# Conv stage: two halves of the gated product and one half of b turned by VectorE blocks and a DRAM round trip

## What is computed

```python
def short_conv_mixer(x, w_in, conv_w, w_out):
    b, c, v = jnp.split(x @ w_in, 3, axis=-1)
    y = b * causal_depthwise_conv(c * v, conv_w)      # 3 taps along the tokens
    return y @ w_out
# h = h + rms_norm(mix); w_in is 1024 x 3072, w_out 1024 x 1024
```

## Time and profile before

| | |
|---|---|
| profiled execution, its own time | 1416.56 us |
| its span, first to last instruction | 1414.8 us |
| median of the timed runs | 1417.77 us |
| PE busy | 1392.3 us, 98% of the span |
| VectorE (DVE) busy | 1026.2 us, 73% |
| ScalarE (ACT) busy | 1011.9 us, 72% |
| GpSimd (POOL) busy | 68.9 us, 5% |
| granted TensorE clock, mean | 0.999 |
| conv stage, its part of the span | about 500 to 585 us |

### The profile page before, as it was taken

The page is one execution under the profiler, slowest core; times in us unless marked ns, Lnnn a source line. Parts: engine busy times, 40 slices in busy tenths (PEclk is TensorE's granted clock), DMA queues, the critical chain, the costliest instruction groups (busy, mean ns, idle before and its releaser), DMA issues.

```text
span 1414.8 us, 20634 instructions
## 1 busy us (share of the span) xinstructions
PE 1392.3 (98%) x7859; PEld 1142.9 (81%) x7859; DVE 1026.2 (73%) x1417; ACT 1011.9 (72%) x1826; POOL 68.9 (5%) x163
## 2 busy tenths in 40 slices
PE   6999999999999999999999999999999999999998
PEld 5888888888888887788887888887778888788886
DVE  5878788777666766676667766677989886876665
ACT  7657574748777554587875977767888886588784
POOL 8000000000000000000000000001030300000000
PEclk9999999999999999999999999999999999999999
DMA  7542453345656555565655565646453432566562
GB/s 234 166 142 91 145 200 121 119 149 180 201 186 206 180 190 181 158 207 188 205 181 179 195 202 185 203 157 194 129 163 112 118 123 90 165 208 200 187 206 91
DMA packets 168291, 238.27 MB, mean 168 GB/s; under 512 B 21554, under 2 KB 114640, under 8 KB 168192
## 3 DMA queue, kind: packets, MB, share of 16 engines
q1 hardware_dynamic: 166496, 233.57, 51.1%
q0 software_dynamic: 1632, 3.35, 0.8%
q10 hardware_dynamic: 64, 0.02, 0.0%
HBM read 235.07 MB, written 1.84 MB: 167 GB/s over the span
## 4 chain that ended last, share of the span: by engine, by line
PE 93%; ACT 3%; DVE 2%; DMA 1%; issue 1%; SPq 0%; DVEq 0%; ACTq 0%
PE A L245 17%; PE A L246 17%; PE A L247 17%; PE M L247 5%; PE G L246 5%; PE M L246 5%; PE G L247 5%; PE M L245 5%; PE G L245 5%; PE A L1325 1%; PE G L1246 1%; PE G L1293 1%; DVE tmp L414 1%; PE M L1303 1%; ACT w_hi L209 1%; DVE x_lo L419 1%
## 5 line engine op out<-in xcount | busy, mean ns | idle before, releaser
L227 DVE TENSOR_TENSOR w_lo<-raw,w_hi 128x1024 fp32r<-128x1024 f32 (+2 forms) x296 | 506.8, 1726 | 128.7 <-ACT w_hi L209 128.0
L209 ACT ACTIVATE w_hi<-raw 128x1024 fp32r<-128x1024 f32 (+2 forms) x296 | 426.7, 1462 | 120.9 <-DMA raw<-in_ffn_w_gate_up 93.3
L245 PE MATMUL A<-w_hi,x_hi 128*128 128x512 f32 (+1 forms) x640 | 258.7, 404 | 3.6 <-DVE x_lo L419 1.0
L247 PE MATMUL A<-w_hi,x_lo 128*128 128x512 f32 (+1 forms) x640 | 247.1, 386 | 0.0
L246 PE MATMUL A<-w_lo,x_hi 128*128 128x512 f32 (+1 forms) x640 | 246.5, 385 | 0.0
L690 ACT ACTIVATE ffn_ffn_hT<-ffn_ffn_hb 32x128 f32<-32x128 f32 x576 | 176.9, 307 | 15.6 <-DVE ffn_ffn_hb L755 2.5
L245 PEld LDWEIGHTS A<-w_hi,x_hi 128*128 128x128 f32 x640 | 120.2, 188 | 33.5 <-DVE x_lo L419 6.8
L247 PEld LDWEIGHTS A<-w_hi,x_lo 128*128 128x128 f32 x640 | 120.1, 188 | 25.1
L245 PE MATMUL A<-w_hi,ffn_ffn_hT_hi 128*128 128x512 f32 x352 | 139.0, 395 | 0.0
L246 PE MATMUL A<-w_lo,ffn_ffn_hT_hi 128*128 128x512 f32 x352 | 138.4, 393 | 0.0
L246 PEld LDWEIGHTS A<-w_lo,x_hi 128*128 128x128 f32 x640 | 120.5, 188 | 21.0 <-issue 0.7
(11 more groups left out here) (392 smaller groups left out, 2018.5 us busy)
## 6 DMA issues: line engine op xcount, KB each, us to landing
raw<-in_ffn_w_gate_up SPq DMA_DIRECT2D x176, 512.0 KB, 4.8
raw<-in_ffn_w_down SPq DMA_DIRECT2D x88, 512.0 KB, 4.0
raw<-in_w_in SPq DMA_DIRECT2D x48, 512.0 KB, 4.2
raw<-in_gdn_w_in SPq DMA_DIRECT2D x48, 512.0 KB, 4.6
raw<-in_sc_w_in SPq DMA_DIRECT2D x24, 512.0 KB, 4.3
raw<-in_w_out SPq DMA_DIRECT2D x16, 512.0 KB, 4.5
raw<-in_gdn_w_out SPq DMA_DIRECT2D x16, 512.0 KB, 4.0
raw<-in_w_mem_kv SPq DMA_DIRECT2D x8, 512.0 KB, 5.9
```

What stands on the lines that cost most here:

```text
L209: ins = act.activation(net.w_hi[:, v % RING, part], net.raw[:, v % RING, part], ACT.Copy)
L227: ins = dve.tensor_tensor(net.w_lo[:, v % RING, part], net.raw[:, v % RING, part], net.w_hi[:, v % RING, part].bitcast(F32), ALU.subtract)
L245: pe.matmul(out, xh, hi[:, k, c, :], start=start and k == 0, stop=False)
L247: mm = pe.matmul(out, xl, hi[:, k, c, :], start=False, stop=stop and k == nk - 1)
```

## The change

Three of the four turns leave TensorE: c*v of both halves and b of half 0. For each of them VectorE turns the 32x32 blocks of the tile in place (new step `tb`, one instruction on 128x1024 elements); GpSimd then writes the tile to a scratch tensor in DRAM (512 KB, 4 KB a partition), waits for it, and reads it back with four DMAs, one for each 32 partitions, each of 1024 runs of 32 floats, which puts the blocks in place. ScalarE's and VectorE's taps and the product with b then read SBUF instead of the banks G and M. The step order changes: `turncv:0` moves behind unit 7, `mul:0` into v1, `turncv:1` behind unit 11 and still ahead of `b:1`. The fourth turn (b of half 1) stays on TensorE but is made in the middle of unit 12, between its second and third quarter, and TensorE's wait for `b_out(2)` moves there with it; units 12 and 13 are written as quarters for this. ScalarE's `b:1` waits for `y(2)` instead of `b_turned(2)`, VectorE's `cv:1` for `tapped(2)` and its own chain.

```diff
+        self.by_blocks = [("cv", 0), ("b", 0), ("cv", 1)]
+        self.blocks, self.turned_in, self.turned_out = s("blocks"), s("turned_in"), s("turned_out")
+        self.turned_dram = net.scratch_dram(f"{name}_turned", [len(self.by_blocks), P, TT * 512])
...
-        steps = "unit:c:0:0 unit:c:0:1 c:0 unit:v:0:0 unit:v:0:1 cv:0 unit:b:0:0 turncv:0 unit:b:0:1 b:0 " \
-                "unit:c:1:0 turnb:0 mul:0 unit:c:1:1 c:1 unit:v:1:0 unit:v:1:1 cv:1 unit:b:1:0 turncv:1 " \
-                "unit:b:1:1 b:1 turnb:1 mul:1 out"
+        steps = "unit:c:0:0 unit:c:0:1 c:0 unit:v:0:0 unit:v:0:1 cv:0 tb:cv:0 unit:b:0:0 unit:b:0:1 b:0 tb:b:0 " \
+                "unit:c:1:0 unit:c:1:1 turncv:0 c:1 unit:v:1:0 mul:0 unit:v:1:1 cv:1 tb:cv:1 unit:b:1:0 unit:b:1:1 " \
+                "turncv:1 b:1 turnb:1 mul:1 out"
...
-        self.b = net.sb("sc_b", [P, TT, 512])
-        self.cvs = net.sb("sc_cv", [P, TT, 512])
+        self.b = net.sb("sc_b", [P, 4, TT, P])
+        self.cvs = net.sb("sc_cv", [P, 4, TT, P])
...
     def pool(self, pool):
         self.post.pool(pool)
+        for n, (what, half) in enumerate(self.by_blocks):
+            tile = self.cvs if what == "cv" else self.b
+            pool.wait_ge(*self.blocks(n + 1))
+            pool.dma_start(self.turned_dram[n], tile[:, :, :, :].rearrange("p k t n -> p (k t n)"))\
+                .then_inc(self.turned_out.sem, 16)
+            pool.wait_ge(*self.turned_out(16 * (n + 1)))
+            src = self.turned_dram[n].rearrange("(i c) (m b n) -> b c m i n", i=4, b=4, n=32)
+            for b in range(4):
+                pool.dma_start(tile[32 * b:32 * b + 32, :, :, :].rearrange("p k t (i n) -> p (k t) i n", i=4), src[b])\
+                    .then_inc(self.turned_in.sem, 16)
+
+    def arrived(self, what, half):
+        return self.turned_in(64 * (self.by_blocks.index((what, half)) + 1))
...
+            elif kind in ("turncv", "turnb") and (kind[4:], int(step[1])) in self.by_blocks:
+                continue
+            elif kind in ("turncv", "turnb") and step != ("turnb", "1"):
+                self.turn(pe, kind, int(step[1]))
             elif kind == "out":
                 pe.wait_ge(*self.cv(2))
-                pe.wait_ge(*self.b_out(2))
                 for h in range(2):
-                    pe.wait_ge(*self.y_lo_ready(h + 1))
-                    w.unit(self.y_hi, self.y_lo, 2 * h, 2, 512, [net.A[0:2], net.A[2:4]], h == 0, False, pieces=2)
+                    for q in range(4):
+                        if (h, q) == (0, 2):
+                            pe.wait_ge(*self.b_out(2))
+                            self.turn(pe, "turnb", 1)
+                        if (h, q) in ((0, 0), (1, 0)):
+                            pe.wait_ge(*self.y_lo_ready(h + 1))
+                        w.unit(self.y_hi, self.y_lo, 2 * h, 2, 512, [net.A[0:2], net.A[2:4]], h == 0, False, pieces=2,
+                               quarter=q)
                 w.last_units(self.post, [(self.y_hi, self.y_lo, 2 * h, self.y_lo_ready(h + 1)) for h in (2, 3)])
...
+    def turn(self, pe, kind, half):
+        net = self.net
+        src, banks, sem, ready = (self.cvs, net.G, self.cv_turned, self.cv) if kind == "turncv" \
+            else (self.b, net.M, self.b_turned, self.b_out)
+        pe.wait_ge(*ready(half + 1))
+        if half:
+            pe.wait_ge(*self.y(2))
+        else:
+            pe.wait_ge(*self.pre.lo(4))
+        for pair in range(2):
+            for kk in range(2):
+                for tt in range(TT):
+                    k = 2 * pair + kk
+                    mm = pe.transpose(banks[pair][:, kk * T + tt * P:kk * T + (tt + 1) * P],
+                                      src[:, k, tt, :], net.ident[:, :])
+            mm.then_inc(sem.sem, 1)
...
+    def turns(self, what, half):
+        return 2 * half if (what, 0) not in self.by_blocks else 0
+
+    def cv_of(self, half, pair):
+        if ("cv", half) in self.by_blocks:
+            return self.cvs[:, 2 * pair:2 * pair + 2, :, :].rearrange("p k t n -> p k (t n)")
+        return self.net.G[pair][:, :].rearrange("p (k n) -> p k n", k=2)
...
                 if kind == "c" and half:
                     act.wait_ge(*self.cv(1))
                 if kind == "b" and half:
-                    act.wait_ge(*self.b_turned(2))
+                    act.wait_ge(*self.y(2))
                 for tt in range(TT):
-                    ins = act.activation((self.c if kind == "c" else self.b)[:, tt, :],
-                                         self.banks(n)[tt][:, :], ACT.Copy, scale=net.r[:, tt:tt + 1])
+                    if kind == "c":
+                        dst, src = self.c[:, tt, :], self.banks(n)[tt][:, :]
+                    else:
+                        dst, src = self.b[:, :, tt, :], self.banks(n)[tt][:, :].rearrange("p (k n) -> p k n", k=4)
+                    ins = act.activation(dst, src, ACT.Copy, scale=net.r[:, tt:tt + 1])
                 ins.then_inc((self.c_out if kind == "c" else self.b_out).sem, 1)
+                moved = ("cv", half) in self.by_blocks
                 for pair in range(2):
-                    act.wait_ge(*self.cv_turned(2 * half + pair + 1))
+                    act.wait_ge(*(self.arrived("cv", half) if moved else self.cv_turned(self.turns("cv", half) + pair + 1)))
...
-                                             net.G[pair][:, kk * T:(kk + 1) * T], ACT.Copy,
+                                             self.cv_of(half, pair)[:, kk, :], ACT.Copy,
...
                 dve.wait_ge(net.unit_used, self.u0 + 2 * (n + 1))
                 dve.wait_ge(*self.c_out(half + 1))
                 if half:
-                    dve.wait_ge(*self.cv_turned(2))
+                    dve.wait_ge(*self.tapped(2))
+                    w.chain.sync()
                 for tt in range(TT):
-                    ins = dve.scalar_tensor_tensor(out=self.cvs[:, tt, :], in0=self.banks(n)[tt][:, :],
-                                                   scalar=net.r[:, tt:tt + 1], in1=self.c[:, tt, :],
+                    ins = dve.scalar_tensor_tensor(out=self.cvs[:, :, tt, :],
+                                                   in0=self.banks(n)[tt][:, :].rearrange("p (k n) -> p k n", k=4),
+                                                   scalar=net.r[:, tt:tt + 1],
+                                                   in1=self.c[:, tt, :].rearrange("p (k n) -> p k n", k=4),
                                                    op0=ALU.mult, op1=ALU.mult)
                     if tt == 0:
                         w.chain.mark(ins)
                 ins.then_inc(self.cv.sem, 1)
+            elif kind == "tb":
+                what, half = step[1], int(step[2])
+                dve.wait_ge(*(self.cv if what == "cv" else self.b_out)(half + 1))
+                w.chain.sync()
+                tile = (self.cvs if what == "cv" else self.b)[:, :, :, :].rearrange("p k t n -> p (k t n)")
+                dve.transpose(tile, tile).then_inc(self.blocks.sem, 1)
...
-                                out=row, in0=net.G[pair][:, kk * T:(kk + 1) * T - back],
+                                out=row, in0=self.cv_of(half, pair)[:, kk, 0:T - back],
...
-                    dve.wait_ge(*self.b_turned(n + 1))
-                    dve.tensor_tensor(t, t, net.M[pair][:, :], ALU.mult).then_inc(self.y.sem, 1)
+                    if ("b", half) in self.by_blocks:
+                        dve.wait_ge(*self.arrived("b", half))
+                        b = self.b[:, 2 * pair:2 * pair + 2, :, :].rearrange("p k t n -> p (k t n)")
+                    else:
+                        dve.wait_ge(*self.b_turned(self.turns("b", half) + pair + 1))
+                        b = net.M[pair][:, :]
+                    dve.tensor_tensor(t, t, b, ALU.mult).then_inc(self.y.sem, 1)
```

More of the change, by code:

```diff
@@ L1775, in pe @@
                 w.unit(net.x_hi, net.x_lo, 4 * h, 4, 512, [[b0], [b1]], h == 0, h == 1)
-            elif kind in ("turncv", "turnb"):
-                half = int(step[1])
-                src, banks, sem, ready = (self.cvs, net.G, self.cv_turned, self.cv) if kind == "turncv" \
-                    else (self.b, net.M, self.b_turned, self.b_out)
-                pe.wait_ge(*ready(half + 1))
-                if half:
-                    pe.wait_ge(*self.y(2))
-                else:
-                    pe.wait_ge(*self.pre.lo(4))
-                for pair in range(2):
-                    for kk in range(2):
-                        for tt in range(TT):
-                            k = 2 * pair + kk
-                            mm = pe.transpose(banks[pair][:, kk * T + tt * P:kk * T + (tt + 1) * P],
-                                              src[:, tt, k * P:(k + 1) * P], net.ident[:, :])
-                    mm.then_inc(sem.sem, 1)
+            elif kind in ("turncv", "turnb") and (kind[4:], int(step[1])) in self.by_blocks:
+                continue
+            elif kind in ("turncv", "turnb") and step != ("turnb", "1"):
```

(1 more changed line is left out.)

## The result

The changed kernel takes 1427.15 us, median of 4 runs (1426.23 to 1429.58), against 1417.89 (1417.53 to 1418.14) for the kernel before, measured beside it: a ratio of 1.0073, 95% interval 1.006 to 1.0085. It is slower by 9.3 us, on the side to which the prediction gave 0.39, and just outside its range.

What follows compares the result with a forecast made beforehand. TensorE (PE), 93% of the chain, bounds the kernel. A 4.4 us wait for b1 eats the 4.2 us gained, leaving +0.3; a 0.9 us slow restart makes +1.2, so 1419.0 us. Range 1415 to 1420.5; 8 in 10: 1414 to 1427.

Steps and rivals of the forecast that it cites:

- parts 1 and 2: PE, conv stage: three turns gone (2.61 us) and b1's turn inside unit 12, hiding its copy; together 4.2 us ahead.
- A: Moment when half 1 of c*v is back from DRAM, before ScalarE's taps; forecast 562.4, break-even 562.1.
- The replay of the queues: Engine steps in the conv stage, replayed with two turns (1.74 us) gone: half 1's block-turned tile ready at 550.8.
- Both have cover, 4.4 and 2.2 us: Half 0's trips of c*v and b return before ScalarE and VectorE need them; b's cover ends beyond a 13.8 us trip.
- weights of unit 11 have 0.9 us to spare: Small reads share DMA engines with weights; unit 11's weights could land 0.9 us later without delaying ScalarE.
- weights stream at the same time here as there, so 3.9: Each trip's 512 KB write to DRAM was taken as 3.9 us, from 512 KB loads on the same queue.
- I take half, 0.9: PE's slow restart after the 4.4 us wait for b1: between nothing and 1.8 us, taken as 0.9.
- the ruler: End of unit 13 on PE, 574.2 before the change; the change is worth whatever it does to that moment.
- (b): Rival: runs of 128 B set the trip's pace, 16.3 us; b0 2.5 late, time 1427; chance 0.39.
- (c): Rival: reads delay unit 10's or 11's weights beyond 0.9 us spare; 1420 at 2 us late; chance within forecast's 0.40.
- (a): Rival: the DRAM trip is short, 7.4 us; 4.0 us gained, time 1413.8; chance 0.16.
- (d): Rival: the wait for b1 inside unit 12 is hidden anyway, only if A < 558; same as (a), no separate chance.

Runs made afterwards that it cites:

- e1: Kernel before with only b1's turn moved inside unit 12, no DRAM trips or block transposes: 1414.69 us, ratio 0.9993.
- e2: Changed kernel with DRAM trips for half 0 only; c*v of half 1 is turned on PE behind unit 10: 1415.26 us, ratio 0.9987.
- e5: Changed kernel with each trip's reads in whole rows of 4 KB instead of 128 B pieces (output not the reference's): 1419.09 us, ratio 1.0007.
- e10: Changed kernel with `mul:0` moved behind `cv:1` and its block transpose: 1425.56 us, ratio 1.0064.
- e9: e2 with `mul:0` moved behind `cv:1` on ScalarE and VectorE: 1415.07 us, ratio 0.998.
- e11: Changed kernel with the order swaps of e7 and e10 together, all three trips kept: 1420.77 us, ratio 1.003.
- e4: Changed kernel with 40 unused matmuls put ahead of TensorE's wait for b1 to keep it busy: 1424.68 us, ratio 1.0053.
- e6: e3 with the last trip's write and four reads issued by ScalarE instead of GpSimd: 1431.94 us, ratio 1.0099.
- e3: Changed kernel with ScalarE's copy of b1 placed ahead of the taps that wait for the trip: 1424.46 us, ratio 1.0055.
- e7: e3 with the splits of units 14 and 15 also ahead of the taps: 1421.54 us, ratio 1.003.

## Why the prediction was wrong: the mechanism held, its sizes did not

**PE's own work (parts 1 and 2) was right.** On before's scale PE's last matmul before the wait ends at 562.74 + 0.39 - 2.3 = 560.8, forecast 560.9. e1 and e2 show the gains alone: 1.63 of 1.5 to 1.6, and 2.95 with two of the three turns gone. e2 also isolates the loss: only half 1's trip is taken back there, and the stage falls from 103.44 to 93.39. That trip, with the wait on it, is what turns a gain of 2.95 into a loss of 7.1.

**The wait stands where it was put.** One wait inside unit 12, ended by ScalarE's copy of b1, behind the taps; from A to PE's restart 572.34 - 569.39 = 2.95, forecast 2.9. The replay of the queues is right too, as long as b and the weights are in time: in e5 the block-turned tile was ready at 550.4, forecast 550.8.

**First failed step: "Both have cover, 4.4 and 2.2 us".** Half 0's b took from 530.33, when its turned tile was ready, to 546.89: 16.6 us, not 11.6, and beyond the 13.8 that I had named as the limit. Of it the write took 4.56 (forecast 3.9) and, above all, the last read landed 9.08 after its issue (forecast 4.2). The cover of c*v, the other of the two, held; b's did not. `mul:0` waited 2.71, and by the step that was named for this case A moved: the tile of half 1 was ready at 553.3, 2.5 late. I had worked out one trip length, from rows with one stream of weights beside them, and used it in a stretch where c*v's reads, b's write and weights fill the engines: the DMA share there is 0.94 to 0.99 in the windows view of the changed kernel from 523 to 547. The trace of before gives the same stretch (521 to 545) a share of 0.55, and b's reads alone took 2.8 us of all 16 engines.

Beside it "weights of unit 11 have 0.9 us to spare" failed as well: they came 2.6 us late. The changed kernel hides it behind b's lateness; e10, e9 and e11 uncover it. So b's trip alone would have moved A by 1.0, and the two together by 2.5.

**Second: "weights stream at the same time here as there, so 3.9".** The third trip's write took 6.04. It was issued 0.9 behind a pair of weight loads, and the table shows how much that place is worth: 2.9 to 6.0 for the same write. Its reads were right as a whole: 2.34 to the last issue (forecast 2.9) and 4.80 to land (forecast 4.2), 7.1 each way. The trip came to 13.8 against 11.6, 2.2 more. A became 567.1 in place of 562.4: 2.5 + 2.2 = 4.7.

**Third: "I take half, 0.9".** The upper bound was 1.8, counted against the 1.09 of a turn after a short pause. Counted the same way the slow restart cost 1.94 - 1.09 = 0.85 on the transposes and, with seven matmuls at 0.43 in place of 0.23, 1.4 more: 2.3 us. Against a running turn's 0.87 it is 2.5. (The prediction set a timeline row, 1.97, beside that 0.87 of the chain; like for like it is 1.97 against 1.03.) e4 shows it goes when PE is kept busy.

Sum: forecast +1.2, plus 4.7, plus 1.6 is 7.5; measured 7.1 by the stage and 7.4 by the ruler. The median lies 0.15 us above the range's end of 1427, and without the 2.2 us outside the stage it would lie inside.

**The rivals.** (b) has the right numbers: its trip of 16.3 is b's 16.6, its delay of 2.5 is there, its unit 13 ends at 581.7, as measured, and its 1427 is the time. In part that is luck. Its A of 569.6 lies 2.5 above the measured 567.1, which the restart makes up for, part of the delay is (c)'s, and 2.2 of the 9.3 us lie outside the stage. Its mechanism is half right. GpSimd's issue is not how the pieces do it: a read takes 0.78 from one issue to the next, less even than the 0.95 forecast. What they cost is time of the DMA engines, 2.9 us against 1.9 for the same 512 KB (e5). With whole rows 6.6 of the stage's 7.1 us are gone, but 3.1 us of A's 6.1 are the place of the last write and not the pieces, so how much of the loss is theirs is not shown; b's trip, and 2.8 us of the last one's reads, are.

The Trainium skill, DMA: Bandwidth & Descriptors, "Specifications", wants 512 B or more in a piece for full rate; the trace agrees, with the 2.9 against 1.9. By the formula of the Trainium skill, DMA: Bandwidth & Descriptors, "Anatomy of one DMA — SWDGE (gpsimd) path", the prediction had a write of 3.2, a last read of 2.3 and an estimated trip of 9.0. The runs stand above it: the write took 2.9 to 6.2, the last read 4.8 to 10.6, and even e5's last trip, with nothing but whole rows, 10.5.

(a) and (d) needed a trip below 8.5; none that was waited for came near. (c) had its condition met: in the changed kernel the weights of unit 11 were late by more than their 0.9, hidden behind b.

**What stays open.** What sets the length of the last trip. The table has it at 11.3 to 15.3, by the write's place among the weight loads and by the reads, which are long where the write is short (e4) and where they meet the next stage's weights (e6). One might think that the trips yield to the weights and end with them: unit 15's weights land at 562.9 to 565.0 on before's scale, the first six trips at 565.2 to 567.4. Two things are against it: e6's trip came back at 573.5 with these weights there at 564.2, and unit 11's weights do lose to a trip. It needs a run in which the weights of units 12 to 15 are asked for earlier or later. Open too are the 1.7 to 4.1 us that the kernels with three such trips take outside the stage.

**Where the gain lies.** Of the kernels run, e9 (0.998, 0.9972 to 0.9989) and e2 (0.9987, 0.9978 to 0.9995) beat both: trips for half 0, whose results are wanted late, and PE for half 1, whose result is wanted at once. Between these two the intervals don't tell; by the stage they are alike, 2.84 and 2.95 us shorter than before. Set against the median of the kernel before beside them, their medians show less, 1.6 (e9) and 1.0 (e2); the intervals of both ratios hold the stage's value as well.

## What to carry to other kernels

A detour through DRAM is bought with slack at the point where its result is wanted, so size each trip for its own stretch, from how full the DMA engines are there, and not one trip for all. Count as well what the trip does to the loads that share its stretch: here it made unit 11's weights 2.6 us late, which only showed once the first delay was out of the way (e10). Before a wait is added, list what stands behind it on that engine: here b1's copy, then the splits, then y_lo of half 1 came up one after the other (e3, e7), and only the third was the product's own work. And count a wait on PE as its length plus a restart.

## What the runs showed of the hardware that I had not expected

PE's slow restart does not need a long wait. Matmuls start 0.43 apart after waits of 2.7 (e11), 3.1 (e5) and 3.3 us (e7) as well, seven or eight of them, some 1.5 us lost. In e5 the granted clock is still 1.00 while the 8 transposes run in 1.06 us (564.4 to 565.6) and 0.50 behind them (566 to 569). After 9.2 us, and after the 8.1 of e3, PE was slow from the first instruction. After the 1.3 of the kernel before there was none. And the changed kernel has the same slow matmuls between 78.6 and 82.4, with no wait at all ahead of them.

The same read of 128 KB in pieces of 128 B, issued by the same engine, landed 4.80 us after its issue in one place and 9.08 in another, and 10.59 in e7; the same write of 512 KB took 2.9 (e5) to 6.2 (e2). The 512 KB loads of unit 11's weights, asked for while b's reads ran, took 8.0 from issue to landing, against 5.0 in the kernel before.

VectorE's block transpose of 1024 columns took 1.25 us as estimated, and the taps from SBUF 494 ns against 475 from PSUM: the parts off the path cost what the rows of before said.
